# A two-block transformer in one core: the first block's layer norms in two token halves, with a shifted one-pass variance

## What is computed

```python
for l in range(2):
    h = x @ w_in[l]                       # kr, c (cq and ckv), fq, fk, fv, ... are column groups of h
    ...                                   # four kinds of attention, concatenated into mix
    y = group_rmsnorm(mix, mix_g[l]) @ w_o[l]
    x = layernorm(ALPHA * x + y, ln1_g[l], ln1_b[l])
    f = (silu(x @ w_gate[l]) * (x @ w_up[l])) @ w_down[l]
    x = layernorm(ALPHA * x + f, ln2_g[l], ln2_b[l])
```

## Time and profile before

| | before |
|---|---|
| median of 3 runs | 3623.53 us (3623.15 to 3624.11) |
| span of the profiled execution, first to last instruction | 3609.5 us |
| outside that span, against the median | 14.0 us |
| PE / DVE / ACT / POOL busy, share of the span | 96% / 44% / 19% / 65% |

### The profile page before, as it was taken

How to read it: one execution, slowest core, us unless ns; L and a number is a source line. 1 busy time by engine, 2 the same in 40 slices (tenths; PEclk the granted TensorE clock), 3 DMA queues, 4 the chain that set the end, 5 groups by cost and what they waited for, 6 DMA issues and landing times.

```text
span 3609.5 us, 41977 instructions
## 1 busy us (share of the span) xinstructions
PE 3463.7 (96%) x14430; PEld 2654.1 (74%) x14430; DVE 1597.8 (44%) x1864; ACT 698.1 (19%) x1380; POOL 2346.8 (65%) x1046
## 2 busy tenths in 40 slices
PE   8999899989988999989999999999999999999998
PEld 6756688868556888768888758888888887578886
DVE  4554311134555111165524856552355338665532
ACT  2242211022342110031101232110111102221110
POOL 6602577757204777748877707887788777258874
PEclk9997899989988999989999969999999999699999
DMA  4200122222101222212223202222222232112221
GB/s 161 76 1 24 65 94 95 96 83 88 36 1 53 93 93 94 95 57 93 93 94 108 88 12 88 93 93 94 94 93 93 93 108 88 35 65 93 93 93 64
DMA packets 82012, 286.31 MB, mean 79 GB/s; under 512 B 9531, under 2 KB 13020, under 8 KB 81628
## 3 DMA queue, kind: packets, MB, share of 16 engines
q1 hardware_dynamic: 76032, 275.81, 22.7%
q10 hardware_dynamic: 5852, 8.78, 0.7%
HBM read 280.89 MB, written 3.67 MB: 79 GB/s over the span
## 4 chain that ended last, share of the span: by engine, by line
PE 69%; DVE 4%; issue 2%; ACT 1%; DVEq 0%; ACTq 0%
PE bank_v L329 13%; PE bank_v L330 13%; PE bank_v L331 13%; PE bank_a L329 7%; PE bank_a L330 7%; PE bank_a L331 7%; PE bank_s L551 2%; PE bank_v L463 2%; PE bank_a L439 1%; PE bank_s L368 1%; PE bank_s L553 1%; PE bank_s L376 1%; DVE lru_x L1439 0%; DVE lru_x L1446 0%; PE bank_s L476 0%
## 5 line engine op out<-in xcount | busy, mean ns | idle before, releaser
L301 POOL TENSOR_TENSOR w_hi<-raw,zero 128x1024 fp32r<-128x1024 f32 x520 | 996.1, 1916 | 1186.5 <-PE bank_v L331 930.1
L304 POOL TENSOR_TENSOR w_lo<-raw,w_hi 128x1024 fp32r<-128x1024 f32 x520 | 1350.8, 2598 | 40.8
L329 PE MATMUL bank_v<-xn_hi,w_hi 128*128 128x512 f32 x1408 | 565.5, 402 | 13.5 <-DVE xn_lo L1024 13.4
L329 PE MATMUL bank_a<-xn_hi,w_hi 128*128 128x512 f32 x1360 | 544.3, 400 | 23.7 <-DVE xn_lo L1086 15.1
L330 PE MATMUL bank_v<-xn_lo,w_hi 128*128 128x512 f32 x1408 | 559.3, 397 | 0.0
L331 PE MATMUL bank_v<-xn_hi,w_lo 128*128 128x512 f32 x1408 | 559.1, 397 | 0.0
L330 PE MATMUL bank_a<-xn_lo,w_hi 128*128 128x512 f32 x1360 | 540.1, 397 | 0.0
L331 PE MATMUL bank_a<-xn_hi,w_lo 128*128 128x512 f32 x1360 | 540.0, 397 | 0.0
L331 PE MATMUL bank_v<-h_hi,w_lo 128*128 128x512 f32 x1056 | 417.7, 396 | 0.0
L329 PE MATMUL bank_v<-h_hi,w_hi 128*128 128x512 f32 x1056 | 417.6, 396 | 0.0
L330 PE MATMUL bank_v<-h_lo,w_hi 128*128 128x512 f32 x1056 | 417.6, 396 | 0.0
(11 more groups left out here) (290 smaller groups left out, 3707.9 us busy)
## 6 DMA issues: line engine op xcount, KB each, us to landing
raw<-in_w_stream SPq DMA_DIRECT2D x520, 512.0 KB, 3.3
rope<-in_rope ACTq DMA_DIRECT2D x2, 1024.0 KB, 6.0
da_v<-t_rows ACTq DMA_DIRECT2D x2, 1024.0 KB, 6.1
out<-resid SPq DMA_DIRECT2D x4, 512.0 KB, 2.6
t_rows<-t_row ACTq DMA_DIRECT2D x1, 1536.0 KB, 6.9
resid<-in_x SPq DMA_DIRECT2D x4, 256.0 KB, 3.8
resid<-in_x ACTq DMA_DIRECT2D x4, 256.0 KB, 9.1
mla_v<-in_alibi ACTq DMA_DIRECT2D x2, 512.0 KB, 6.9
```

The source lines that it names most:

```text
L301: pool.tensor_tensor(w_hi[:, u, :], raw[:, u, :], zero[:, 0:1].to_broadcast([P, UNIT]), ALU.add).then_inc(*hi_split.done(("unit", u)))
L304: pool.tensor_tensor(w_lo[:, u, :], raw[:, u, :], w_hi[:, u, :].bitcast(F32), ALU.subtract).then_inc(*w_split.done(("unit", u)))
L329: pe.matmul(out, lhs_hi, rhs_hi, start=first, stop=False)
```

## The change

Lines of the changed kernel are its own. In words:

- **A shift instead of the mean.** Chunks 0 and 1 of the sum ALPHA * x + y are added (L1271), PE spreads that sum after the third output unit (`ln_shift_sum`), and its negated mean over 256 channels, `ln_shift`, is added to all chunks: to 0 and 1 afterwards (L1275), to the others in `base` (L1210) before the bank is added in `evict` (L1217).
- **Sums as chunks come.** A running sum `ln_sum` (L1225) and a running sum of squares `ln_squares` (L1233; ACT squares into `ln_square`). `ln_stats` sums both over channels with four matmuls of 256 columns for one half of the tokens, with the last chunk's values taken straight from `resid` and `ln_square`.
- **Halves.** `wo` 6 and 7 (for `ln2`, chunk 7 of `down`) are run for tokens 0 to 255 and then for 256 to 511. The factors of a half are 128 x 256 tiles made by DVE and ACT (`factors`: mean, variance, root, reciprocal, offset), and the normalised value is resid * rstd + offset (two DVE steps, L1254 and L1258), then gain and bias twice on ACT, once into `xn_hi` and once into `resid`, then `xn_lo` (L1127) on DVE.
- **Weaving.** The first four units of the next stage (`gate0` 0, `up0` 0, `gate0` 1, `up0` 1; after `ln2` and at the start `kr`, `c` 0, `c` 1, `fk` 0) are run by `project_halves`: half by half, chunk by chunk, the second pair of units four chunks behind the first. Their slots are all released at the end of the second half. The input split at the start is made in halves too.

```diff
+LN_HALVED = dict(ln1=DC - 2, ln2=DC - 1)
...
-            def variance(tag):
-                for c in range(0, DC, 2):
-                    pe.wait_ge(*added.after((tag, "pair", c)))
-                    token_sums((tag, "pair", c), squares[:, c, :], c // 2 * TT)
-                spread(tag)
-            def down(tag):
+            def ln_stats(tag, s):
+                cut = HALVES[s]
+                b = bank_s[1 + s]
+                pe.wait_ge(*added.after(ln_key(tag, DC - 2, s, tag, "sum")))
+                pe.matmul(b[:, HALVES[0]], ones[:, :], ln_sum[:, cut], start=True, stop=False)
+                pe.wait_ge(*v_read.after(ln_key(tag, DC - 1, s)))
+                pe.matmul(b[:, HALVES[0]], ones[:, :], resid[:, DC - 1, cut], start=False, stop=True)
+                pe.wait_ge(*added.after(ln_key(tag, DC - 2, s, tag, "squares")))
+                pe.matmul(b[:, HALVES[1]], ones[:, :], ln_squares[:, cut], start=True, stop=False)
+                pe.wait_ge(*squared.after(ln_key(tag, DC - 1, s, tag)))
+                pe.matmul(b[:, HALVES[1]], ones[:, :], ln_square[:, (DC - 1) % 2, cut], start=False, stop=True
...
+                used = [unit(("wo", c)) for c in (DC - 2, DC - 1)]
+                for s, cut in enumerate(HALVES):
+                    for c, u in zip((DC - 2, DC - 1), used):
+                        b = v_bank(("wo", c, s))
+                        for k in range(DC):
+                            mm = mm3(b[:, cut], *w_tile(u, k), xn_hi[:, k, cut], xn_lo[:, k, cut], k == 0, k == DC - 1)
+                        mm.then_inc(*(w_used.done(("wo", c)) if s else sums.done(("wo", c, s))))
+                        if s == 1 and c == DC - 2:
+                            ln_stats(tag, 0)
...
+            def project_halves(pairs, wait, lag, between=None):
...
+                for s, cut in enumerate(HALVES):
+                    for n in range(DC + lag):
+                        for p, pair in enumerate(pairs):
+                            c = n - p * lag
+                            if not 0 <= c < DC:
+                                continue
+                            if p == 0:
+                                pe.wait_ge(*wait(c, s))
+                            for key, bank in pair:
+                                if key not in units:
+                                    units[key], banks[key] = unit(key), bank(key)
+                                mm = mm3(banks[key][:, cut], *w_tile(units[key], c), xn_hi[:, c, cut], xn_lo[:, c, cut],
+                                         c == 0, c == DC - 1)
+                                if s == 1 and c == DC - 1:
+                                    mm.then_inc(*w_used.done(key))
+                        if between and s == 0 and n == lag:
+                            between()
+            def down(tag, norm=None):
                 for c in range(DC):
...
+                    halves = HALVES if norm and c == DC - 1 else (slice(0, S),)
...
+                            if s == 1 and f == 8:
+                                ln_stats(norm, 0)
+                    if norm and c == 2:
+                        ln_shift_sum(norm)
+                if norm:
+                    ln_stats(norm, 1)
...
-                project("kr", v_bank, lambda c: x_lo.carried(("in1", c), ("ln2", c)))
-                for n in range(3):
-                    project(("c", n), a_bank)
+                project_halves(((("kr", v_bank), (("c", 0), a_bank)), ((("c", 1), a_bank), (("fk", 0), v_bank))),
+                               lambda c, s: x_lo.carried(("in1", c, s), ("ln2", c, s)), 4)
+                project(("c", 2), a_bank)
...
-                for c in range(DC):
-                    project(("wo", c), v_bank, is_split("mixnorm") if c == 0 else None)
-                mean("ln1")
-                variance("ln1")
-                ffn("ffn", is_split("ln1"))
-                mean("ln2")
-                variance("ln2")
+                project_out("ln1")
+                project_halves([[(("ffn", "gate0", k), a_bank), (("ffn", "up0", k), v_bank)] for k in range(2)],
+                               lambda c, s: x_lo.after(("ln1", c, s)), 4, lambda: ln_stats("ln1", 1))
+                ffn_rest("ffn")
+                down("ffn", "ln2")
...
+                def apply(s):
+                    cut = HALVES[s]
+                    factors(s)
+                    for c in range(DC):
+                        gain, bias = par1[:, g + c:g + c + 1], par1[:, b + c:b + c + 1]
+                        act.wait_ge(*scaled.after((tag, c, s)))
+                        act.activation(xn_hi[:, c, cut], resid[:, c, cut], ACT.Identity, scale=gain, bias=bias
+                                       ).then_inc(*x_hi.done((tag, c, s)))
+                        act.activation(resid[:, c, cut], resid[:, c, cut], ACT.Identity, scale=gain, bias=bias
+                                       ).then_inc(*affine.done((tag, c, s)))
+                        if s == 0 and c == 1:
+                            square_of(DC - 1, 1)
+                for c, s in ln_parts(tag)[:-1]:
...
+                def base(c):
+                    dve.scalar_tensor_tensor(out=resid[:, c, :], in0=resid[:, c, :], scalar=ALPHA, in1=ln_shift[:, :],
+                                             op0=ALU.mult, op1=ALU.add).then_inc(*dve_step.done((tag, "base", c)))
...
+                def factors(s):
+                    cut, b = HALVES[s], bank_s[1 + s]
+                    dve.wait_ge(*sums.after((tag, "stats", s)))
+                    step(dve.tensor_scalar(mean[:, cut], b[:, HALVES[0]], 1.0 / D, None, ALU.mult), (tag, "mean", s))
+                    step(dve.tensor_scalar(rstd[:, cut], b[:, HALVES[1]], 1.0 / D, 1e-5, ALU.mult, ALU.add),
+                         (tag, "square", s))
+                    dve.wait_ge(*act_step.after((tag, "mean2", s)))
+                    dve.tensor_tensor(var[:, cut], rstd[:, cut], var[:, cut], ALU.subtract).then_inc(*dve_step.done((tag, "var", s)))
+                    dve.wait_ge(*rooted.after((tag, s)))
+                    step(dve.reciprocal(rstd[:, cut], var[:, cut]), (tag, "rstd", s))
+                    step(dve.scalar_tensor_tensor(out=offset[:, cut], in0=mean[:, cut], scalar=-1.0, in1=rstd[:, cut],
+                                                  op0=ALU.mult, op1=ALU.mult), (tag, "offset", s))
+                def apply(s, after_two=None):
+                    cut = HALVES[s]
+                    for n in range(DC + 3):
+                        if n < DC:
+                            dve.tensor_tensor(resid[:, n, cut], resid[:, n, cut], rstd[:, cut], ALU.mult
+                                              ).then_inc(*dve_step.done((tag, "times", n, s)))
+                        if 1 <= n <= DC:
+                            dve.wait_ge(*dve_step.after((tag, "times", n - 1, s)))
+                            dve.tensor_tensor(resid[:, n - 1, cut], resid[:, n - 1, cut], offset[:, cut], ALU.add
+                                              ).then_inc(*scaled.done((tag, n - 1, s)))
+                        if n >= 3:
+                            dve.wait_ge(*affine.after((tag, n - 3, s)))
+                            split_lo_half(tag, n - 3, s)
+                        if n == 1 and after_two:
+                            after_two()
+                for c in range(2):
...
+                dve.wait_ge(*sums.after((tag, "shift")))
+                step(dve.tensor_scalar(ln_shift[:, :], bank_s[0][:, :], -1.0 / (2 * P), None, ALU.mult), (tag, "shift"))
+                for c in range(2):
+                    dve.tensor_tensor(resid[:, c, :], resid[:, c, :], ln_shift[:, :], ALU.add).then_inc(*centered.done((tag, c)))
+                base(2)
+                late = LN_HALVED[tag] < DC - 1
+                for c, s in ln_parts(tag)[2:-1]:
+                    evict(c, s)
+                    if s != 1 and c < DC - 1:
+                        base(c + 1)
+                    if 3 <= c < DC - 1:
+                        add_sum(c, s)
+                    if s is None or c == DC - 2:
+                        if s != 1:
+                            add_square(c - 1, None)
+                    if c == (DC - 1 if late else DC - 2):
+                        add_square(DC - 2, s)
+                factors(0)
+                def last_part():
+                    evict(DC - 1, 1)
+                    if late:
+                        add_square(DC - 2, 1)
+                apply(0, last_part)
+                factors(1)
+                apply(1)
...
-        out += _proj_units(np.concatenate([cut["cq"], cut["ckv"]], 1))
-        for name in ("fq", "fk"):
-            out += _proj_units(cut[name])
...
+        c, fk = _proj_units(np.concatenate([cut["cq"], cut["ckv"]], 1)), _proj_units(cut["fk"])
+        out += [c[0], c[1], fk[0], c[2]] + _proj_units(cut["fq"]) + [fk[1]]
```

## The result

The changed kernel took 3627.99 us (median of 20 runs, 3625.55 to 3633.99), the kernel before 3623.84 (20 runs). The ratio is 1.0015, interval 1.0009 to 1.0021: **slower by 4 us by the medians, by 5 (3 to 8) by the ratio**, where 12 us less were forecast. The time lies in the stated range and on the other side of no change.

A forecast was written before the change was run, and what follows sets the result against it. PE, busy 3463.7 of 3609.5 us, was taken as the bound, so time is won only where it waits. Terms: 2 x 1.7 + 8.5 - 2 + 2 = 12, so 3623.5 - 12 = 3611.5 us, range 3588 to 3634.

The forecast's parts named there:

- The step that failed: Start of each layer, latent norm's chain: its sums, with fewer units behind them, have 1.3 us to spare, costing nothing.
- The rule as the prediction told it: DVE instructions with two SBUF inputs lock out POOL's reads and vice versa; those with at most one mostly don't contend.
- ln1: Norm after attention, both layers: products end 7.1 us or more later, weaving wins it back, gain 1.7 us each.
- First ln2: First layer's norm after `down`: no waits, first woven matmul 10.4 us after the products, gain 8.5 us.
- Last ln2: Final norm, nothing woven: loss 2 us, ending at T + 32.2 against 30.4, T being the old products' end.
- Start: Input split and first units in halves: three units end at 48.8 instead of 51.0, gain 2 us.
- Matmuls of 256 columns: PE: half-size matmuls follow one another every 0.11 us, half of 0.233, so products cost the same in halves.
- Steps of 256 columns: DVE steps on token halves from SBUF take 0.345 us in a row, 1.03 us per chunk of three.
- the rival of halves that aren't half: DVE steps of 256 columns cost 0.425 us in a row, chunks every 1.27; 3625 us, no difference; chance 0.20.
- the one of the clock: Woven matmuls wait for chunks, clock stays low some 17 us instead of 4 to 5; 3633 us; chance 0.15.
- the fast rival: In the norms POOL holds DVE up hardly at all; 43.5 us gained, time 3580 us; chance 0.12.
- The 14.0 us outside the span: Profiled execution's 3609.5 us plus 14.0 around it give the median 3623.5; what lies around should stay.

The follow-up runs named there:

- e6: The changed kernel run again without any edit, for a second profile: 3629.18 us, ratio 1.0016 to the kernel before.
- e4: e2 with ln1's running sums over chunks 3 to 5 added only after output unit 6's first half is evicted: 3605.04 us, ratio 0.9952.
- e2: The changed kernel with the latent norm's eight diagonals made by ACT instead of DVE: 3618.59 us, ratio 0.9978 to the kernel before.
- e1: The changed kernel with the latent norm's token sums one unit earlier on PE, its root before the second fq eviction: 3625.66 us, ratio 1.0001.
- e8: e5 with a further unused tile of 16 columns, so that the activations start at byte 106176: 3558.61 us, ratio 0.9824.
- e5: e4 with the half's factors made from PSUM and a new one-column epsilon tile that moves the tiles behind it: 3538.78 us, ratio 0.977.

## Why the prediction was wrong

**The step that failed** is the one edit that was costed at nothing: "its sums have 1.3 us to spare by my count: nothing." It measured 7.9 us in the first layer (fifth unit at 50.93 against 50.79, first matmul of 384 columns at 130.49 against 122.50) and 6.7 in the second, 14.5 us together. Of the 7.9, 4.6 are the two waits and the rest is mostly the low clock behind them; in e6, with the same waits and a clock of 0.68 instead of 0.50 from 81 to 86 us, it is 6.6. This alone turns 12 faster into 3 slower. The chain behind the sums was counted rightly but for one price. Its reciprocal ended at 71.3; with the 2.54 us that the eight diagonals took before, they would have been there at 73.9, 1.3 us before the products of the one covering unit, `fk` 1, ended. They took 9.66. In the kernel before POOL had a gap of 3.00 us at that point, with slots released one by one; with four slots released within a few us it had none from 46.44 to 83.2. The lock itself had been found, priced from the earlier trace rows and applied to every step of the norms; it was not applied to steps that the change doesn't touch, but beside which it moves POOL's work. The Trainium skill, "SBUF — State Buffer", section "Who interferes with whom", counts `tensor_scalar` with the operations that can take the shared port for the whole instruction; the diagonals (up to 2.43 us beside POOL, 0.27 in its gap) agree. The rule as the prediction told it, for steps with two SBUF inputs, would not have named them: they have one tile and a column. The trace of before had the sign, the first of the eight at 1.17 us.

Term by term, from the table and the timelines:

- **ln1** 1.7 each forecast; 2.0 each (fifth unit at 428.26, with 7.27 us of delay brought along, against 423.07). Right, its waits nearly so: 0.27, 0.45 and 2.99 against 0.5, 0.8 and 3.2. e4 showed that the cause of the last is the third locked step per unit. The 8.40 before the first woven matmul has luck in it: only variance and offset waited for POOL (1.62 and 2.18 us), while the first product and addition, forecast to wait as well, ran in 0.42 each, and other steps of DVE filled the time.
- **First ln2** 8.5; 6.3 (817.55 and 818.6, with 5.3 brought along). The mechanism is right, the size off: DVE evicts the second half of chunk 7 only after the offset and two `times` steps, each behind POOL (2.01, 2.00 and 2.56 us), and an addition, PE waits 6.66 us for it, and the first woven matmul comes 13 us after the products, not 10.4.
- **Last ln2** loss 2; 2.0. Right. (The sum gives T + 32.0, not 32.2.)
- **Start** gain 2; none (0.1 later at the fifth unit). The 16 half steps took 15.00 us behind POOL where 7 whole ones took 13.19, and PE's second half ran to 50.2.
- **Matmuls of 256 columns** 0.11, "half of 0.233"; 0.118 in the woven units. Half of 0.233 is 0.117.
- **Steps of 256 columns** 0.345 in a row; 0.335, with a duration of 0.42. So the rival of halves that aren't half (0.425 in a row) didn't come, nor the one of the clock: from 399.30 to 404.30 the changed kernel has a mean clock of 0.51, then 1.00, as here:

```profile
399.30:404.30 5.00, 5.00 (x24) 5.00 (x25) 4.50 (x14) 5.00 (x12) 0.00 (x0) 0.51 0.00 0
404.30:406.30 2.00, 2.00 (x17) 1.95 (x17) 0.85 (x2) 1.05 (x3) 0.00 (x0) 1.00 0.00 0
```

Sum of what was measured: 4.0 + 6.3 - 0.1 - 2.0 = 8.2 faster, against 12 by the same four terms, less 14.5 for `lat`: 6.3 slower, where the stages have 5 to 8. e2, which takes `lat` out, is at 3618.6, so the forecast's world does exist and is worth some 5 to 8 us by the runs (8.5 to 9.8 by the stages) rather than 12. That the time fell within the stated range is owed to the range's width; its low end, 3588, lies three quarters of the way to the fast rival and not half.

**The 14.0 us outside the span** were no such thing (1.8 are outside; of the other 12.2, 10.6 were a higher clock in the second attention). It didn't enter the sum, which is a difference, but the line should have warned: no row showed anything that takes 14 us outside the span.

## What to carry to other kernels

- Where a change moves the work of an engine that locks another out, re-price every step of the locked one in that stretch, also those that the diff doesn't touch, and above all the short chains that had stood in a gap.
- Releasing several buffers at once turns a refill with gaps into one without; what used to run in the gaps must get another engine (the diagonals on ACT, e2) or another time (the sums when POOL is idle, e4).
- Before tuning waits of a few us in a kernel bound by matmuls, compare the pace of a matmul with the tiles moved by an unused column; one that brought them to a multiple of 128 bytes was worth 60 to 70 us here, more than all the rest. Compare each shape: those of 256 columns did not gain.

## What the hardware showed that was not expected

The pace of a 512-column fp32r matmul goes with the start address of its moving operand, the tile of 512 columns (`xn`, `h`): 0.2333 us at 32 bytes over a multiple of 64, 0.2289 at 64 over a multiple of 128, 0.2267 at a multiple of 128, all at a granted clock of 1.00. Only tiles behind the inserted column moved; `w_hi`, `w_lo`, `raw` and `resid` stayed, so the moving operand is the only SBUF operand of these matmuls that moved. That its address is the cause is inferred from this; the tiles that other engines use beside PE moved too, and no run moved `xn` or `h` alone.

Other shapes behave otherwise in the same traces. The woven matmuls of 256 columns became slower in the place that is best for 512: 0.1183 us each at 106080, 0.1199 at 106112. Those with the weights as the moving operand, whose stationary operand `xn` moved, went from 0.1167 to 0.1198 at 256 columns and stayed at 0.1734 at 384. There is a further influence that no run isolates: with no tile moved, the latter were at 0.1178 in e1 (256 columns) and 0.1767 in e4 (384), and e8 has its 144 at 0.2333.

And the attention stage of one and the same program takes 200.8 to 217.1 us, along with a mean clock of 0.90 to 0.81, from one layer and execution to the next. The best kernel of the study, e5 (halves, diagonals on ACT, late sums, factors from PSUM, activations at a multiple of 128), is at 0.977 of the kernel before (0.9751 to 0.9788), and at 3538.78 it is also below the kernel before with the gap alone (3553.84).
